# Stream attention as parts between the steps of the channel stage, with low weight halves written over the raw ones

## What is computed

```python
h = modulate(rms_norm(x), sh1, sc1)
proj = h @ w_in                       # pooling input, q, k, v, forget gates
# streams: attention of 16 new rows over 1024 cached rows and themselves
s = einsum('bqhd,bkhd->bhqk', q, k_all) * HEAD_DIM ** -0.5
s = s + fq[..., :, None] - fk[..., None, :]      # cumulative log-forget bias
att = softmax(where(mask, s, -inf)) @ v_all
x = x + g1 * (concat(pool_y, att) @ w_out)
h2 = modulate(rms_norm(x), sh2, sc2)
x = x + g2 * (square(relu(h2 @ w_up)) @ w_down)
```

## Time and profile before

| | |
|---|---|
| median of three runs | 3449.24 us |
| profiled execution | 3458.4 us, its span 3456.8 us |
| PE busy | 3136.6 us (91%) |
| DVE, ACT, POOL busy | 61%, 45%, 11% |
| HBM read and written | 409.65 and 90.13 MB |
| stream attention, first load to the channel stage's first load | 1445.68 to 1661.70 us |
| prologue of the channel stage, to the first up step | 1661.70 to 1774.75 us |
| channel stage's end | 3456.8 us |

### The profile page before, as it was taken

One profiled execution on the slowest core, in us unless ns is written; L12 is line 12 of the kernel. 1 busy time (PEld: TensorE's weight loads), 2 busy tenths in 40 slices (PEclk: granted clock), 3 DMA queues, 4 the chain that ended last, 5 costly groups with the idle time before them and its releaser, 6 DMA issues.

```text
span 3456.8 us, 47686 instructions
## 1 busy us (share of the span) xinstructions
PE 3136.6 (91%) x17260; PEld 2685.9 (78%) x17260; DVE 2119.2 (61%) x3214; ACT 1549.6 (45%) x2576; POOL 368.6 (11%) x326
## 2 busy tenths in 40 slices
PE   4999998569999999788569999999999999999998
PEld 2999998148877878655458887888889888888997
DVE  3655664548977879633354555655565566567554
ACT  2344443058877878533233333333433344344432
POOL 0000000111211111211030012100220021012001
PEclk7999999679999999888779999999999999999999
DMA  5567565853524332298523333423444354344342
GB/s 192 195 213 244 186 232 180 265 151 82 132 70 119 82 94 71 84 312 266 183 103 103 110 110 117 158 94 115 139 140 133 131 175 159 131 162 175 124 134 92
DMA packets 319606, 514.81 MB, mean 149 GB/s; under 512 B 24784, under 2 KB 249560, under 8 KB 312857
## 3 DMA queue, kind: packets, MB, share of 16 engines
q1 hardware_dynamic: 302701, 450.67, 40.6%
q0 software_dynamic: 16704, 61.62, 5.1%
HBM read 409.65 MB, written 90.13 MB: 145 GB/s over the span
## 4 chain that ended last, share of the span: by engine, by line
PE 46%; DVE 2%; issue 1%; POOL 1%; ACT 1%; DMA 0%; SPq 0%; POOLq 0%; DVEq 0%; ACTq 0%
PE c_psd L2175 24%; PE c_psu L2164 22%; DVE c_acc L2089 1%; PE c_pst L2185 0%; DMA c_dn_raw<-in_w_out_dram 0%; DVE c_dn_lo L2059 0%; POOL c_x L1907 0%; POOL c_x L1910 0%; SPq L1875 0%; DVE c_hT L2114 0%; DVE c_up_lo L2054 0%; ACT c_dn_hi L1990 0%; DVE c_x L2105 0%; POOL c_acc L1920 0%; DMA c_xin<-x 0%
## 5 line engine op out<-in xcount | busy, mean ns | idle before, releaser
L2164 PE MATMUL c_psu<-c_hT,c_up_hi 128*128 128x384 f32 (+1 forms) x2560 | 707.5, 357 | 2.5 <-DVE c_hT L2114 2.5
L2164 PEld LDWEIGHTS c_psu<-c_hT,c_up_hi 128*128 128x128 f32 x2560 | 471.7, 188 | 46.6 <-issue 2.8
L2175 PE MATMUL c_psd<-c_dn_hi,c_a_hi 128*128 128x512 f32 x1360 | 425.3, 394 | 41.2 <-DVE c_a_lo L2064 14.8
L2164 PE MATMUL c_psu<-c_hT,c_up_lo 128*128 128x384 f32 (+1 forms) x1280 | 457.0, 357 | 0.0
L2089 DVE TENSOR_TENSOR c_acc<-c_psd,c_acc 128x1024 f32<-128x1024 f32 x255 | 310.7, 1221 | 211.5 <-PE c_psd L2175 210.5
L2175 PE MATMUL c_psd<-c_dn_lo,c_a_hi 128*128 128x512 f32 x1360 | 421.8, 391 | 0.0
L2175 PE MATMUL c_psd<-c_dn_hi,c_a_lo 128*128 128x512 f32 x1360 | 420.8, 391 | 0.0
L2001 ACT ACTIVATE c_relu<-c_psu 128x384 f32<-128x384 f32 (+1 forms) x160 | 84.8, 530 | 627.3 <-PE c_psu L2164 627.3
L2071 DVE TENSOR_TENSOR c_a_lo<-c_relu,c_a_hi 128x384 fp32r<-128x384 f32 (+1 forms) x160 | 112.2, 702 | 377.9 <-ACT c_a_hi L2006 377.8
L632 PE MATMUL p_psm<-p_whi,p_hT_hi 128*128 128x384 f32 (+1 forms) x952 | 322.7, 339 | 16.9 <-DVE p_wlo L525 10.2
L2175 PEld LDWEIGHTS c_psd<-c_dn_hi,c_a_hi 128*128 128x128 f32 x1360 | 253.3, 189 | 96.9 <-DVE c_acc L2089 15.8
(11 more groups left out here) (229 smaller groups left out, 5171.3 us busy)
## 6 DMA issues: line engine op xcount, KB each, us to landing
c_up_raw<-in_w_up_dram SPq DMA_DIRECT2D x80, 1024.0 KB, 5.4
c_dn_raw<-in_w_down_dram SPq DMA_DIRECT2D x80, 1024.0 KB, 4.8
p_raw<-in_w_in_dram SPq DMA_DIRECT2D x24, 1536.0 KB, 7.2
s_krows<-in_cache_k_dram SPq DMA_DIRECT2D x16, 1536.0 KB, 6.6
s_vrows<-in_cache_v_dram POOLq DMA_DIRECT2D x16, 1536.0 KB, 7.6
c_dn_raw<-in_w_out_dram SPq DMA_DIRECT2D x20, 1024.0 KB, 4.9
o_wm<-in_w_mod_dram SPq DMA_DIRECT2D x16, 1024.0 KB, 7.0
q_split<-p_split SPq DMA_DIRECT2D x34, 384.0 KB, 2.3
```

What stands on the lines that cost most here:

```text
L2164: last = pe.matmul(ps_u[g][:, 0:w], weights[j % 2][:, k, f], x[:, k, 0:w], start=(k == 0 and n == 0), stop=(k == KT - 1 and n == 2))
L2175: last = pe.matmul(ps_d[n % 2][:, half, :], a[u % 2][:, g, cols], weights[u % 2][:, g, 512 * half:512 * (half + 1)], start=(g == 0 and j = ...
```

## The change

`stream_attention` is removed as a stage. Its work is cut into 116 parts (`stream_parts`): for each half of the heads a set-up (queries and new keys of all streams are transposed) and the first new-key scores, and for each of 16 units (half, stream) the parts keys 0, 1, 2 (8 transposes each), scores, turn (the probabilities' transposes), values, and out together with the next unit's new-key scores. `PART_AFTER` places one part behind each step of the step list, from the first out step on, except behind steps next to the turn and to down 14 of a block. The last part stands behind step 123 of 0 to 180 (block 3, down 4). On every engine a part's work follows the step's own.

Keys and values of a unit share one buffer, `kv`: the keys' transposes are copied back over the keys, and the values are loaded over them after the scores. The bias is loaded right into `probs`, in one buffer. The parts use the eight bank slots of `ps_t`, which the norm's transposes use too; PE waits (`banks_free`) before a part for the part before it to have been copied out. SP issues a part's loads two steps later in its order, behind a wait for that part:

```diff
+            def stream_loads(what, u, a):
+                s, m = divmod(u, STREAMS)
+                if what == "setup":
+                    sp.wait_ge(S["turned0"], u + 1)
+                    load_keys(STREAMS * u)
+                elif what == "scores":
+                    sp.wait_ge(S["scored"], u + 1)
+                    load_values(u)
+                elif what == "turn":
+                    sp.wait_ge(S["p_turned"], 2 * u + 2)
+                    if u + 1 < UNITS:
+                        load_bias(u + 1)
+                elif what == "values":
+                    sp.wait_ge(S["valued"], u + 1)
+                    if u + 1 == UNITS:
+                        load_stream_mods()
+                    elif m == STREAMS - 1:
+                        load_stream_rows(s + 1)
+                    else:
+                        load_keys(u + 1)
...
             for n, at in enumerate(STEP_LIST):
                 if at[0] == "up":
...
+                two_before = n - 2 if ("turn", 0, 0) not in STEP_LIST[n - 2:n + 1] else n - 3
+                for part in PART_AFTER.get(two_before, ()) if at[0] != "turn" else ():
+                    stream_loads(*part)
```

To make room, the weights' buffers change. There are now two raw buffers for up and two for down and out, and the two low halves lie on them; the subtraction is done in place. A load waits for the matmuls that last used the buffer, no longer for the low half:

```diff
-        up_raw = sb("c_up_raw", [P, KT, G * P])
+        with ExitStack() as same:
+            up_lo = [same.enter_context(nc.sbuf_tensor(f"c_up_lo{i}", [P, KT, G * P], F32R)) for i in range(2)]
+            dn_lo = [same.enter_context(nc.sbuf_tensor(f"c_dn_lo{i}", [P, G, D], F32R)) for i in range(2)]
+        up_raw = [sb(f"c_up{i}", [P, KT, G * P]) for i in range(2)]
+        dn_raw = [sb(f"c_dn{i}", [P, G, D]) for i in range(2)]
...
             def load_up(b, s):
-                wait_past(sp, up_ready, up_no(b, s))
+                j = up_no(b, s)
+                wait_past(sp, up_done, G * (j - 1))
...
-                wait_past(sp, dn_ready, u)
+                wait_past(sp, tile_done, BEFORE[max(u - 1, 0)])
```

What PE does in the parts:

```diff
+            def stream(what, u, a):
...
+                elif what == "keys":
...
+                    for half in range(2):
+                        for i in range(4 * half, 4 * half + 4):
+                            last = pe.transpose(ps_t[:, i, :], kv[:, i, P * a:P * a + P], ident[:])
+                        last.then_inc(S["k_turned"], 1)
+                elif what == "scores":
+                    for half, bank in enumerate((bank0, bank1)):
+                        for a in range(SPAIRS):
+                            last = pe.matmul(bank[SPR * a:SPR * a + SPR, :], qd[:, a, m, :],
+                                             kv[:, 4 * half:4 * half + 4, P * a:P * a + P], start=True, stop=True,
+                                             tile_position=(0, SPR * a))
+                    last.then_inc(S["scored"], 1)
```

More of the change, by code:

```diff
@@ L1727 @@
 CHUNKS_OUT = KT // G
[L1728 removed]
+OUT_AFTER = [None] + [(4, 6, 8, 10)] * (NG - 2) + [(5, 7, 9, 11)]
 STREAM_TILE = QT
@@ L1756, in up_no, with stream_parts, near_turn, part_before @@
     return STEPS * b + s
+SR = HG * NEW
+SPR = 2 * NEW
+SPAIRS = HG // 2
+SCT = PAST // P
+SKEYS = PAST + NEW
+UNITS = 2 * STREAMS
+def stream_parts():
+    for s in range(2):
+        yield (("setup", s, 0),)
+        yield (("new", STREAMS * s, 0),)
+        for u in range(STREAMS * s, STREAMS * (s + 1)):
+            for a in range(SPAIRS):
+                yield (("keys", u, a),)
+            yield (("scores", u, 0),)
+            yield (("turn", u, 0),)
+            yield (("values", u, 0),)
+            yield (("out", u, 0), ("new", u + 1, 0)) if u % STREAMS < STREAMS - 1 else (("out", u, 0),)
+def near_turn(n):
+    return any(at[0] == "turn" or at[:1] + at[2:] == ("down", STEPS - 2) for at in STEP_LIST[n:n + 2])
+PARTS = list(stream_parts())
+PART_AFTER = dict(zip([n for n in range(len(STEP_LIST)) if not near_turn(n)], PARTS))
+OUT_STREAMS = STEP_LIST.index(("out", NG - 1, 0))
+assert len(PART_AFTER) == len(PARTS) and max(PART_AFTER) < OUT_STREAMS - 1, (len(PART_AFTER), len(PARTS), max(PART_AFTER), OUT_STREAMS)
+def part_before(n):
+    return PART_AFTER[max(m for m in PART_AFTER if m < n)]
 def norm_steps(b, after):
@@ L1975, in steps @@
                     since, coming = 0, at[1]
+                for part in PART_AFTER.get(n, ()):
+                    stream(*part)
         @block.scalar
@@ L2188, in _ @@
             pe.wait_ge(ident_ready, 1)
-            for at in STEP_LIST:
+            for n, at in enumerate(STEP_LIST):
                 kind, b, s = at
+                if kind == "turn" or kind == "down" and s == STEPS - 2:
+                    for part in part_before(n):
+                        banks_free(*part)
                 if kind == "up":
@@ L2207, in _ @@
                             turn(b + 1, i)
+                for i, part in enumerate(PART_AFTER.get(n, ())):
+                    if i == 0 and n > min(PART_AFTER):
+                        for before in part_before(n):
+                            banks_free(*before)
+                        turns = [FIRST[b + 1] if k == "turn" else FIRST[b + 2] for k, b, s in STEP_LIST[:n]
+                                 if k == "turn" or k == "down" and s == STEPS - 2 and b + 1 < NG]
+                        if turns:
+                            pe.wait_ge(hT_ready, turns[-1])
+                    stream(*part)
 def build(nc, ins, outs):
```

506 lines of the change are left out of this document (211 added, 295 removed).

## The result

The changed kernel takes 3579.03 us (median of four, 3574.85 to 3585.02) against 3447.84 us (3437.13 to 3454.27) for the kernel before beside it: a ratio of 1.038, 95% interval 1.036 to 1.040, so 131 us slower. The direction of the forecast was right; its size, +51 us, was not, and 3579 lies outside the range of 3425 to 3550. In the two profiled executions, on which the sum was made, the span went from 3456.8 to 3573.2 us, +116.4.

The account below looks back on a forecast made before the run. PE was taken to bound the channel stage. 3456.8 - 216.0 (stage) + 123.2 (parts) + 80.8 (thirteen places) + 22.1 (clock) + 36.5 (smaller waits) + 4.7 (prologue) = 3508.1 us of span, so 3500 us measured; range 3425 to 3550.

Parts of the forecast that it names:

- loss of clock: Channel stage: PE waits of 5 to 7 us lower the granted clock, 1.7 us at each of 13 places, +22.1 us.
- thirteen places: Down or out steps, four tiles, blocks 0 and 1: late weights make PE wait 7.0 or 5.3 us before tile 3, +80.8.
- the last unit: 24 rows of stream modulation issued ahead of a weight load: PE waits 5.7 us, with the clock 8.
- smaller waits: Late weights around up steps, out steps after a freed buffer and the last unit: together +36.5 us.
- the change between parts and weight matmuls: PE's switch between weight matmuls and each of 116 parts: taken as 0, at most 36 us.
- The bound: Channel stage is PE-bound, 351 of 355 us busy in its first block, so inserted PE work is paid in full.
- Removed stage and prologue: Stream attention stage gone, -216.0 us; channel stage's prologue, where out 2 and 3 loads wait for PE, +4.7 us.
- Parts on PE: Stream work inserted in PE's order: 7.54 us for each of 16 units plus 2.6, +123.2 us, 2.7 in the prologue.
- (a): Rival: stream data don't hold back the weights, which land 5 us after the part; 3405 us, chance 0.12.
- (b): Rival: everything is hidden because DVE and ACT run ahead of PE; 3356 us, chance 0.04.
- (c): Rival: PE pays more per part, or lateness piles up over steps; 36 us or more on top, 3537 us, chance 0.10.
- (d): Rival: the change does not do what it says, e.g. streams' results wanted before they are ready; chance 0.04.

Follow-up runs that it names:

- y1: Changed kernel with both edits, weights issued ahead of SP's wait for a part (x1) and low half made behind the last take (x4): 3385.17 us.
- y2: x1 with the eight key transposes of each keys part done twice, 384 more of them: 3440.32 us.
- z2: Kernel before, stream stage kept, with the change's new weight buffers and the low half made behind the step's last take: 3462.56 us.
- x1: Changed kernel, but SP issues each step's weights ahead of its wait for a stream part: 3404.05 us.
- x2: Changed kernel with only the first of eight row blocks of keys and values loaded from the second unit on: 3503.02 us.
- x4: Changed kernel with DVE making the low half behind the step's last take, not behind tile 0: 3466.91 us.
- y3: x1 with three small DVE reductions ahead of tile 3's bank at fourteen down steps of four tiles, making PE wait: 3424.31 us.
- y4: x1 with seven small DVE reductions ahead of tile 3's bank at fourteen down steps of four tiles, making PE wait: 3479.89 us.
- z1: Changed kernel with the keys' and values' loads issued by ACT's queue, SP keeping its waits and the weights: 3529.01 us.

## Why the prediction was right or wrong

**The steps that failed.** The order of events was forecast rightly, the time wasn't: three terms of the sum were too small. The largest is the loss of clock, +22.1 us for thirteen places and 2.3 at the last unit, where the windows show 52 us behind 24 waits; then the smaller waits, +36.5 us against 62.6; then the change between parts and weight matmuls, taken as 0, which costs 15. The paragraphs below go through the terms in turn.

**The bound: right.** The parts are paid in full (y1, y2), the rest of the difference is PE waiting and a lower clock.

**Removed stage and prologue: nearly right.** Up to the first up matmul the new kernel is 213.3 us shorter (1774.7 to 1561.4). The forecast had -216.0 + 4.7 + 2.7 = -208.6. From the stage's first load the prologue was 2.6 us longer than forecast (123.0 against 113.0 + 7.4); that the prompt attention ended 7.3 us earlier in this execution (PE's last matmul of it starts at 1432.26, before at 1439.53) makes up the rest. The second part is luck: the program is the same up to there, and in z2, whose program is too, the next stage's first load stands at 1439.24 where before it stood at 1445.68. The shape was right: four waits of 16.2, 5.1, 7.3 and 6.3 us where there had been 14.8, 13.4 and two of 1.2.

**Parts on PE: too low by 15 us.** 120.5 forecast behind the prologue, 135.6 measured in y1. The change between weight matmuls and parts, bounded by 0 and 36 and taken as 0, costs 0.13 us for each of 116; y1's starts show it in the first weight matmuls behind a part, while the parts themselves took 119.3 us, near the 120.5 forecast. The bound's middle would have been right; that groups of one round follow each other was no row for groups that alternate with the weight matmuls.

**The thirteen places: right, at eleven by the mechanism forecast.** 76.1 us measured, 80.8 forecast; each exists, 3.51 to 7.50 us long. At eleven PE waits before tile 3, as forecast. At two, 3.51 us at 2025.41 (down 13 of block 0) and 6.90 at 2465.30 (down 11 of block 1), it waits before tile 2 for the take of tile 0: the weights of the up step before were late, behind values, and DVE came too late out of that step, which holds norm work too. The landings fit as well: 9.8 and 9.6 us behind values and keys at two of the places (forecast 9.8), 7.7 behind the bias rows at one (8.1); at all but down 11 of block 1, ACT's first copy starts 7.8 to 10.5 us after the step. x1, x2 and x4 confirm the three links one by one: SP's order, the bytes ahead, the low half in front of the take.

**The clock: the term that was mis-sized most.** Forecast 1.7 us at 13 places, 22.1. Measured: after the 24 waits of 2.2 us or more the granted clock over 7 us is 0.57 to 0.79, by the windows 52 us lost in all, 2.2 each: 29.6 at the thirteen places, where 22.1 were forecast, and 22.5 at the eleven others, where 2.3 were. Three of these windows, behind waits of 2.41, 6.83 and 4.94 us, and one behind a wait of 2.00 us (length, PE busy, clock, DMA share, GB/s):

```profile
1654.40:1661.40 7.00, 7.00 (x24) 0.76 0.00 0
1714.20:1721.20 7.00, 6.99 (x30) 0.78 0.04 15
...
2366.70:2373.70 7.00, 6.94 (x19) 0.57 0.00 0
...
2400.22:2407.22 7.00, 6.69 (x33) 1.00 0.00 0
```

I had read the price from two rows at the low end (1.9 and 1.6 us), and outside the thirteen places the forecast counted a loss of clock only at the last unit. Eleven of the 24 waits lie outside, nine of them longer than the 2.8 us that had cost 1.6 us in the earlier trace rows.

**The smaller waits: too low by 26 us.** PE's idle time grew by 138.7; without the thirteen places 62.6, against 36.5 forecast. The largest had been set to zero, at the start of block 2, where one up step follows another (SP, then ACT, then PE):

```profile
2578.50 2.68 SPq L1648 DMA_DIRECT2D s_probs<-nF_s  x6
2581.23 0.42 SPq L1611 DMA_DIRECT2D c_up<-in_w_up_dram  x1
```
```profile
2585.69 1.91 ACT L1823 ACTIVATE c_dn_hi<-c_dn 128x2048 fp32r<-128x2048 f32 x1 [8.43 <-DMA c_dn<-in_w_down_dram]
2587.51 0.47 ACT L1834 ACTIVATE c_relu<-c_psu 128x384 f32<-128x384 f32 x1
```
```profile
2588.12 0.98 PE L2077 MATMUL c_psu<-c_hT,c_up_hi 128*128 128x384 f32 x2 [9.65 <-ACT c_relu L1834]
```

ACT takes the late down weights first and the relu that empties the bank behind them; the forecast followed DVE's takes behind late weights on down steps, and ACT's relu only into the next step, where it was worth 1 to 2 us. Others that weren't forecast, or only as smaller ones: 6.63 us at 2977.19 (the first down step of block 3), 5.51 at 2882.13, 4.29 at 2057.84, 3.92 at 2497.27, and 5.10 at 3090.52, where SP's loads still stand behind the 24 small ones. The wait that these were forecast to cause came out as worked out, 5.59 us at 3077.09 (forecast 5.7), with SP busy 11.72 us on them.

Together: -4.7 (prologue and start) + 15.1 (parts) - 4.7 (thirteen places) + 33 (clock) + 26 (smaller waits) = 65 us, the difference between the 116.4 us of the two spans and the 51.3 forecast. The 33 is what parts and idle time leave of the growth in length, 55.4 us, less 22.1; the windows show 52 of it. The medians differ by 131 since the profiled execution of before lay above its median, and that of after below.

**The rivals.** (a), stream data that hold nothing back, is out: landings of 9 to 10 us, and x2. (b), all hidden, doesn't hold for this kernel, but y1 comes within 13 us of its 3364 us of span (3377.0), about the 15 us that the parts cost more. (c), more per part and lateness that piles up, was right in kind: the first half of it is 15 us, and two late steps in a row gave the 9.65 us. Lateness went from one step into the next also at the two places above. It didn't pile up over many: in order of time the thirteen show no growth (6.20, 6.83, 4.83, ... 6.49, 4.94, 6.90). (d) didn't happen.

## What to carry to other kernels

Ahead of a load that somebody needs, put neither a wait for work just being done nor bytes that are needed later, even where the DMA engines have room: here the order of one queue decided between 1.3% faster and 3.8% slower. When the landing of weights moves, check in which order each engine uses them, ACT's relu as well as DVE's takes, and keep work that frees PE's banks ahead of preparations for later. And count a wait of PE above 2 us at its length and about 2 us more for the clock (a few such waits lost none), at all places and not only at those where the forecast has its large terms.

## What the runs showed of the hardware that I had not expected

- In the changed kernel the waits of PE of 0.9 to 2.0 us lost nothing of the clock, and the 24 of 2.2 us and more lost 1.5 to 3.0 us each, with no clear relation to their length: 9.65 us cost 1.5 and 4.94 us 3.0. The border isn't sharp: behind 1.97 us in y3 and 1.83 us in x4 1.7 us were lost, behind 2.74 us in y3 and three of 3.25 us in y4 none. What tells the cases apart isn't settled.
- A load on a second queue overtakes if its packets are the larger: 1 MB of down weights (4096 bytes a packet) issued together with 1.5 MB of values (1536) landed in 5.7 us, 0.9 us above the 4.8 us of one alone. At another step the out weights came 6.0 us after issue in z1, and 10.3 in the changed kernel. It holds along z1's list: of the 14 down and out loads issued in the same instant as keys or values, 13 land in 5.7 to 7.3 us; of the 11 up loads (1024 bytes a packet), nine land in 8.5 to 9.6 us and none sooner. The counts in z1's windows, 272 packets against 358 and 1040 against 955, fit queues served packet by packet; no run changed the packet size alone.
- A transpose of a key block among the weight matmuls costs 0.10 us (y2), about what it took in the full round of the stream stage. The change back to the weight matmuls costs another 0.10 to 0.16 us a part (y1's medians by kind of step).
